# Where TensorE's expert loop has its turn: between two items, or between an item's first gate tile and the rest

## The reference

```python
def swiglu(x, w_gu, w_down):
    gate, up = jnp.split(x @ w_gu, 2, axis=-1)
    return (jax.nn.silu(gate) * up) @ w_down

def moe_swiglu(xn, w_router, w_gu, w_down):
    logits = (xn @ w_router).astype(jnp.float32)
    top_v, top_i = lax.top_k(logits, TOP_K)
    top_w = jax.nn.softmax(top_v, axis=-1)
    gates = jnp.sum(jax.nn.one_hot(top_i, N_EXPERTS, dtype=jnp.float32) * top_w[..., None], axis=-2)
    out = jnp.zeros(xn.shape, jnp.float32)
    for e in range(N_EXPERTS):
        out = out + gates[..., e:e + 1] * swiglu(xn, w_gu[e], w_down[e]).astype(jnp.float32)
    return out.astype(xn.dtype)
```

## Time and profile before

| | |
|---|---|
| median of three runs | 1516.02 us (1512.35 to 1521.06) |
| the profiled execution | 1516.77 us, its span 1515.1 us |
| TensorE busy | 1428.1 us, 94% of the span |
| first matmul of the expert loop, last one's end | 580.9 us, 1498.2 us |
| granted TensorE clock over the span | 0.966 |

### The profile page before, as it was taken

How to read it: one execution, slowest core, us unless ns; L and a number is a source line. 1 busy time by engine, 2 the same in 40 slices (tenths; PEclk the granted TensorE clock), 3 DMA queues, 4 the chain that set the end, 5 groups by cost and what they waited for, 6 DMA issues and landing times.

```text
span 1515.1 us, 35581 instructions
## 1 busy us (share of the span) xinstructions
PE 1428.1 (94%) x15792; PEld 866.4 (57%) x15792; DVE 435.6 (29%) x645; ACT 317.1 (21%) x507; POOL 149.7 (10%) x219
## 2 busy tenths in 40 slices
PE   8999899999998899998998998998998998998995
PEld 7998799999896584343343343343343343344343
DVE  6864555555557821110110110110110110110111
ACT  5833443443446831000000000000000000000000
POOL 0600010000122715001001001001001001001001
PEclk9999999999998997999999999999999999999998
DMA  9760255555998045999999999999999999999992
GB/s 298 236 200 24 85 168 188 174 178 188 134 294 288 1 164 223 399 418 386 418 410 362 408 407 352 406 406 358 419 408 344 419 410 345 411 410 359 414 418 83
DMA packets 132794, 455.03 MB, mean 300 GB/s; under 512 B 12451, under 2 KB 74108, under 8 KB 132642
## 3 DMA queue, kind: packets, MB, share of 16 engines
q1 hardware_dynamic: 126386, 435.15, 75.2%
q0 software_dynamic: 6080, 17.37, 5.0%
q10 hardware_dynamic: 176, 0.14, 0.0%
HBM read 436.51 MB, written 14.55 MB: 298 GB/s over the span
## 4 chain that ended last, share of the span: by engine, by line
PE 91%; issue 3%; DVE 2%; ACT 2%; DMA 1%; POOL 0%; ACTq 0%; POOLq 0%; DVEq 0%
PE ps L1617 91%; DVE arena L1462 1%; DVE arena L1459 1%; DMA arena<-item_rows,arena 0%; ACT arena L1131 0%; DMA arena<-in_norm_mix_g 0%; ACT x_hi L930 0%; PE ps L1628 0%; PE ps L1865 0%; ACT x_hi L960 0%; DVE arena L1463 0%; ACT between L1152 0%; POOL arena L792 0%; PE ps L1635 0%; ACT arena L1028 0%
## 5 line engine op out<-in xcount | busy, mean ns | idle before, releaser
L1617 PE MATMUL ps<-more,arena 128*32 128x448 f32 x3456 | 328.9, 539 | 0.0
L1617 PE MATMUL ps<-ring,arena 128*32 128x448 f32 x2688 | 275.0, 569 | 31.7 <-issue 30.3
L1586 DVE TENSOR_TENSOR arena<-arena,ps 128x448 f32<-128x448 f32 x48 | 29.8, 621 | 811.0 <-PE ps L1617 807.4
L1617 PEld LDWEIGHTS ps<-more,arena 128*32 128x32 f32 x3456 | 105.8, 110 | 218.9 <-issue 218.9
L1617 PEld LDWEIGHTS ps<-ring,arena 128*32 128x32 f32 x2688 | 85.5, 115 | 213.0 <-issue 211.5
L1617 PE MATMUL ps<-ring,between 128*32 128x256 f32 x3360 | 189.2, 379 | 0.0
L511 DVE TENSOR_TENSOR w_lo<-ring,w_hi 128x2048 fp32r<-128x2048 f32 x67 | 153.3, 2291 | 78.1 <-ACT w_hi L505 78.1
L1617 PEld LDWEIGHTS ps<-ring,between 128*32 128x32 f32 x3360 | 105.5, 110 | 85.8 <-issue 8.1
L505 ACT ACTIVATE w_hi<-ring 128x2048 fp32r<-128x2048 f32 x67 | 127.7, 1911 | 102.8 <-PE ps L1617 96.7
L1617 PE MATMUL ps<-x_hi,w_hi 128*128 128x256 f32 x800 | 113.0, 293 | 9.7 <-ACT x_hi L930 4.4
L1209 ACT ACTIVATE arena<-ps 128x448 f32<-128x448 f32 x48 | 26.1, 544 | 456.5 <-PE ps L1617 456.5
(11 more groups left out here) (260 smaller groups left out, 1072.6 us busy)
## 6 DMA issues: line engine op xcount, KB each, us to landing
more<-in_moe_w_gu SPq DMA_DIRECT2D x144, 896.0 KB, 7.8
ring<-in_moe_w_gu SPq DMA_DIRECT2D x112, 896.0 KB, 7.5
ring<-in_moe_w_down SPq DMA_DIRECT2D x80, 896.0 KB, 7.8
more<-in_moe_w_down SPq DMA_DIRECT2D x48, 896.0 KB, 7.8
ring<-in_ffn_w_gu SPq DMA_DIRECT2D x22, 1024.0 KB, 5.1
ring<-in_a_w_in SPq DMA_DIRECT2D x16, 1024.0 KB, 10.6
ring<-in_ffn_w_down SPq DMA_DIRECT2D x11, 1024.0 KB, 5.0
ring<-in_w_kv SPq DMA_DIRECT2D x6, 1024.0 KB, 5.1
```

The costliest lines, as they stand in the source:

```text
L1586: dve.tensor_tensor(SU[:, a, :], SU[:, a, :], ps[:, b, 0:QUARTER], ALU.mult).then_inc(bank_free[b], 1)
L1617: return pe.matmul(o, w, x, start=start, stop=stop, **kw)
```

## The change

TensorE's loop is laid out anew; the other engines' code is the same. The work of an item is cut in two functions: `first_part` waits for `x_ready` and does the 8 chunks of gate 0, `other_part` does the other 40 chunks. The first part of the first item now stands ahead of the loop. A turn of the loop does the other part of item `i` and then the first part of item `i + 1`. The other part of the last item stands behind the loop. The loop's number of turns is read from `route[ITEMS + 1]`, one less than the number of items. The order of the matmuls and of their waits is the same as before.

```diff
+FIRST_PART = KC
...
             pe.wait_ge(counted, 1)
-            n_items = pe.value_load(route[0:1, ITEMS:ITEMS + 1], min_val=E, max_val=ITEMS - 1)
-            with pe.Fori(0, n_items) as i:
-                def free(name):
...
+            n_before_last = pe.value_load(route[0:1, ITEMS + 1:ITEMS + 2], min_val=E - 1, max_val=ITEMS - 2)
+            def free(i, name):
...
+            def first_part(i):
 
                 pe.wait_ge(x_ready, i + 1)
+                for m, (kind, j, q) in enumerate(ITEM[:FIRST_PART]):
+                    input_chunk(i, m, kind, j, q)
+
+            def other_part(i):
+
                 for m, (kind, j, q) in enumerate(ITEM):
+                    if m < FIRST_PART:
+                        continue
                     if kind != "dn":
-                        input_chunk(m, kind, j, q)
+                        input_chunk(i, m, kind, j, q)
                         continue
                     if q == 0:
                         pe.wait_ge(hidden_turned, i * TILES + j + 1)
                     chunk_arrived(pe, m, i)
                     for r in range(ROWS_DN):
                         if (4 * r + 3) // PIECES == q:
-                            down_row(j, r)
+                            down_row(i, j, r)
+
+            first_part(0)
+            with pe.Fori(0, n_before_last) as i:
+                other_part(i)
+                first_part(i + 1)
+            other_part(n_before_last)
```

More of the change, by code:

```diff
@@ new lines, in _, with input_chunk @@
+            n_before_last = pe.value_load(route[0:1, ITEMS + 1:ITEMS + 2], min_val=E - 1, max_val=ITEMS - 2)
+            def free(i, name):
+                b, k = bank_count(name, i)
+                pe.wait_ge(bank_free[b], k)
+                return b
+            def input_chunk(i, m, kind, j, c):
+                w = chunk_arrived(pe, m, i)
+                for a in range(GROUPS):
+                    b = free(i, (kind, j, a)) if c == 0 else JTURN[(kind, j, a)][0]
+                    for n in range(4):
+                        last = mm(ps[32 * n:32 * n + 32, b, 0:QUARTER], XT[:, a, c, :], w[:, QUARTER * n:QUARTER * n + QUARTER],
+                                  c == 0, c == KC - 1)
+                    if c == KC - 1:
+                        last.then_inc(bank_full[b], 1)
+                if m not in FILLS:
+                    last.then_inc(chunk_used, 1)
@@ new lines, in down_row @@
+            def down_row(i, j, r):
+                first, final = j == 0 and r == 0, j == TILES - 1 and r == ROWS_DN - 1
+                for a in range(GROUPS):
+                    b = JTURN[("y", a // 2)][0]
+                    if first and a % 2 == 0:
+                        free(i, ("y", a // 2))
+                    at = PIECE * (a % 2)
+                    for n in range(4):
+                        q, piece = divmod(4 * r + n, PIECES)
+                        w = chunk_slot(CHUNK_AT[("dn", j, q)])[0]
+                        last = mm(ps[32 * n:32 * n + 32, b, at:at + PIECE], HT[j][:, a, r, :], w[:, PIECE * piece:PIECE * piece + PIECE],
+                                  first and a % 2 == 0, final, skip_group_check=True)
+                    if final and a:
+                        last.then_inc(bank_full[b], 1)
+                if not final and any((4 * r + n) % PIECES == PIECES - 1 for n in range(4)):
+                    last.then_inc(chunk_used, 1)
```

## The result

The changed kernel took 1550.33 us (median of 4 runs, 1547.22 to 1551.37), the kernel before 1516.24 us beside it (4 runs, 1512.35 to 1521.06). The ratio is 1.022, with a 95% interval of 1.0186 to 1.0253. Predicted were 1500 us and a range of 1491 to 1518. What happened is the rival that had 15%, the badly placed head, and on top of it a smaller loss that no rival had by itself.

What follows compares the result with a forecast made beforehand. The prediction took TensorE as the bound, busy 1428.1 of 1515.1 us, with seven loop turns costing 6.61 us each. It summed 1516.8 - 6.6 - 5.4 - 4.7 = 1500.1 us, predicting 1500 us, range 1491 to 1518.

Steps and rivals of the forecast that it cites:

- the badly placed head: Rival, 15%: the loop's first instructions fall near their fetch block's end, so TensorE stalls twice per turn; 1535 us.
- one jump fewer: Term at the loop's branch: seven passes with six jumps instead of eight with seven, saving one turn of 6.6 us.
- six gaps shorter by 0.9: Term for TensorE's idle time at the six remaining turns: gaps shrink from 4.33 to about 3.4 us, saving 5.4 us.
- clock, six times 0.8: Term for the matmuls behind six turns: low-clock loss falls from 2.28 to 1.5 us each, saving 4.7 us.
- GpSimd's rows at the new place: Within a 15% rival: row transfers may be on the way at the moved turn, so turns keep their price; 1509.4 us.
- Cover: At the moved branch, queued 448-column matmuls hide 2.2 us of the jump, where 256-column ones hid 1.36 us.
- only one jump fewer: Rival, 15%: one turn goes, but the other six keep their price at the new place; 1509.4 us.
- Weights just hidden: Per item, weight transfers of about 112.8 us stay within 113.5 us of matmuls and turn; costed at 0.

Runs made afterwards that it cites:

- a_slot0: The changed kernel with only its loop's head set at the first instruction of a fetch block of 256; 1515.1 us, 0.9995 of the kernel before.
- a_old: The changed kernel with the turn put back between two items, the last item still behind the loop; 1511.3 us, 0.9961 of the kernel before.
- a_rows: a_slot0 with GpSimd holding the next item's four token loads until up 0 of the running item is done; 1508.9 us, 0.9947 of the kernel before.
- a_five: The changed kernel with the turn after 5 chunks of an item instead of 8; 1504.1 us, 0.9901 of the kernel before.
- a_up0: The changed kernel with the turn after 16 chunks, between up 0 and gate 1; 1512.8 us, 0.9967 of the kernel before.
- a_dn: The changed kernel with the turn after 28 chunks, between the first half of down 0 and up 1; 1516.8 us, 0.9992 of the kernel before.
- a_pad180: The changed kernel with 180 already met wait instructions added at the start of TensorE's program; 1538.6 us, 1.0138 of the kernel before.

## Why the prediction was wrong, step by step

**The step that failed** is the cost of the moved head, which the sum put at nothing. It stood as a rival at 15% with nothing behind it but the rhythm of the packets, outside the range, and it came to 33.6 us. The rival's own text had what was needed: the head moves by 384 instructions, which is half a block; a second packet follows about 5 us behind the first; a head in the last part of its block stalls twice. What it lacked was where in its block the head of either kernel stands. That can be counted in the compiled program: about 111 before, and 111 + 385 = 496, which is 240, after. With 16 instructions left of 256 this was no matter of chance, and the profile after shows it as six matmuls between two gaps.

That its price came out near (6 x 5.1 = 31 us against 33.6 us) is luck, for two errors cancel. I had 5.1 us more idle time in a turn and the clock as before. The second gaps were 3.7 to 4.3 us each, and the first ones 0.6 us shorter than in a_slot0, so that a turn had 3.3 us more idle time (8.9 against 5.6 us). The lower clock cost 4.1 us a turn instead of 2.0 us. One reading in it was wrong as well: from 812 to 817 us the trace has 28 matmuls, not 46, so by that count fewer instructions ahead of the block's end are enough than the last third that I named.

**The terms of the sum**, by the matmuls from first to last:

| step | predicted | measured |
|---|---|---|
| one jump fewer | -6.6 | -7.6 (917.3 to 909.7, a_old) |
| six gaps shorter by 0.9 | -5.4 | with the next term -0.6 (909.7 to 909.1, a_rows) |
| clock, six times 0.8 | -4.7 | |
| GpSimd's rows at the new place | in a rival, as no gain | +6.0 (909.1 to 915.1, a_slot0) |
| head's place | in a rival, +31 | +33.6 (915.1 to 948.7) |
| sum | -16.7 | +31.4 |

By the ratios in the experiments' table, which rest on 4 to 10 executions each, the same steps are -5.9, -2.1, +7.3 and +34.1 us. The second of them is within the spread, so that the gaps and the clock together saved 0.6 to 2.1 us, and possibly nothing, where I had 10.1 us.

- *One jump fewer*: right, and 0.7 us less than predicted by the ratios, 1.0 us more by the profiled executions. Seven branches, one at 76 ns, no gap behind it, and no gap between down 1 and the next gate 0.
- *Cover*: right as a mechanism and in size (1.4 against 2.3 us, where the earlier trace rows gave 1.36 and 2.2), but the gain was eaten. I subtracted the new cover from the old branch time. The branch at the quiet new place is 6.1 us, at the old one 5.3 us on average, so the gap went from 4.3 to only 4.1 us. The fetch sets out earlier there, as said above; why, no run tried.
- *Clock*: the gain didn't come. I drew a slope through seven turns and took 1.5 us for a gap of 3.4 us. With 3.9 to 5.1 us of idle time (a_five, a_rows, a_up0, a_old, a_dn) the part of a turn that isn't idle was 2.5, 2.4, 2.3, 2.3 and 2.3 us: no slope that a shorter gap could have used. With 5.6 us (a_slot0) it was 2.0 us. The groups that I saw in the earlier trace rows don't go by the gap: in a_up0 the six gaps were all 4.0 to 4.2 us, and the rest of a turn was 1.6 to 3.1 us (see the 7.62 and 6.17 us behind its second and third turn). Since no gap as short as 3.4 us in every turn was made, and three executions of a_five ran 4 to 7 us faster at a higher granted clock, it isn't shown that a shorter gap saves nothing.
- *Branch time at the new place*: the rival "only one jump fewer" named GpSimd's rows, and said they would keep a turn's price. They did: with the head mended, 1515.1 us, some 6 us more than the 1509.4 us of that rival, as the branch got dearer and not only no cheaper.
- *Weights just hidden*: right. No wait for weights shows in any kernel whose branches stall, and the DMA queues stand idle 6 us in a turn of the kernel after. Once the turns are gone the weights bind at 878.5 us, so the most that a cure could bring here is 38.8 us.

The Trainium skill ("Runtime: NRT & Kernel Launch", "Instruction fetch mechanics") states that instructions come in blocks of 256 and that a jump to a target outside the resident ones stalls for a fetch. The trace agrees, with 4.7 to 8.4 us for such a branch, and 0.36 us for one whose target had been announced.

## What to carry to other kernels

When an engine's loop has a body as long as this one (2900 machine instructions), moving its turn moves its head too: count at which instruction of its fetch block the head falls before and after, since 16 instructions left in the block cost here 5.6 us in every turn. Before such a turn is moved to a better place, try to have its target fetched ahead: here a hint took some 6 us off each branch, and made the place, the cover and the head of no account. And a fetch goes over the same DMA engines as the data, so look at which small transfers are on the way when the branch comes.

## What the runs showed of the hardware beyond this

- A wait that is already met is not free at the start of a program. TensorE's 128 extra wait instructions ran from 5.6 to 19.3 us, 180 from 5.2 to 24.5 us and 129 in the other kernel from 5.3 to 19.1 us, 0.11 us each. The expert matmuls started 11.4, 20.2 and 17.5 us later. That isn't proportional, but their start varied between 580.4 and 585.2 us in the kernels without extra waits too.
- A taken branch that goes back 2900 instructions cost 4.7 to 6.3 us with no small packets around, the one more branch that `head_slot` brings at the loop's entry (a_slot0, at 599.8 us) 0.33 us, a branch not taken 0.08 us.
- With the head 165 instructions into its block (a_pad180, by the same count) there was no second gap; between there and 240 no run was made.
- With a stop of TensorE of 3.3 to 6.1 us, the granted clock fell to half in every turn of every kernel. In the straight-line version and the two with the hint, whose stops are 2.5 us at most, it stayed at 1.00 through all the expert matmuls.
